# Splitting the two value projections over the last inverse levels, and reading the first head's sum ahead of the last inverse part

## What is computed

```python
# group A, per chunk of 64 tokens: needs the inverse of a unit lower triangular matrix
L = jnp.where(strict, jnp.einsum("bhncd,bhnsd->bhncs", k_beta, k) * decay, 0.0)
sol = lax.linalg.triangular_solve(L + eye, rhs, left_side=True, lower=True, unit_diagonal=True)
# group B, per head
z = jnp.einsum("bhqd,bhkd->bhqk", q_blk, kh) * scale
log_keep = jnp.where(mask, jax.nn.log_sigmoid(-z), 0.0)
between = lax.cumsum(log_keep, axis=3, reverse=True) - log_keep
weight = jnp.where(mask, jnp.exp(jax.nn.log_sigmoid(z) + between), 0.0)
return jnp.einsum("bhqk,bhkd->bhqd", weight, vh)
```

## Time and profile before

| what | us |
|---|---|
| median of 3 runs | 1599.32 |
| lowest and highest of them | 1590.52, 1599.54 |
| the profiled execution | 1589.53 |
| its span, as the trace has it | 1587.7 |
| TensorE busy in it | 1519.0 |

### The profile page before, as it was taken

One profiled execution on the slowest core, in us unless ns is written; L12 is line 12 of the kernel. 1 busy time (PEld: TensorE's weight loads), 2 busy tenths in 40 slices (PEclk: granted clock), 3 DMA queues, 4 the chain that ended last, 5 costly groups with the idle time before them and its releaser, 6 DMA issues.

```text
span 1587.7 us, 54543 instructions
## 1 busy us (share of the span) xinstructions
PE 1519.0 (96%) x25973; PEld 1334.5 (84%) x25973; DVE 258.1 (16%) x489; ACT 179.0 (11%) x383; POOL 143.7 (9%) x167
## 2 busy tenths in 40 slices
PE   9999999999999999999999999999999998999997
PEld 8787587777687864999999999999999998998996
DVE  3433310000143435100010010010010000000102
ACT  3223120000131332200000000000000000000001
POOL 2334200000022532200000000000000000000000
PEclk9999999999999999999999999999999999999999
DMA  9213344444243135999999999999999999999992
GB/s 329 95 54 134 106 160 159 160 159 147 80 173 107 53 144 207 364 397 373 373 379 369 354 369 376 370 383 368 371 363 377 364 384 359 367 359 369 399 374 97
DMA packets 133612, 433.48 MB, mean 273 GB/s; under 512 B 9082, under 2 KB 33916, under 8 KB 119052
## 3 DMA queue, kind: packets, MB, share of 16 engines
q1 hardware_dynamic: 132384, 427.70, 71.7%
q0 software_dynamic: 672, 2.14, 0.5%
q10 hardware_dynamic: 332, 0.13, 0.0%
HBM read 428.89 MB, written 1.05 MB: 271 GB/s over the span
## 4 chain that ended last, share of the span: by engine, by line
PE 92%; issue 3%; DVE 2%; ACT 1%; POOL 1%; DMA 0%; ACTq 0%; DVEq 0%
PE ps L1130 35%; PE ps L1154 18%; PE ps L979 9%; PE ps L681 8%; PE ps L990 4%; PE ps L844 3%; PE ps L692 3%; PE ps L1187 2%; PE ps L801 1%; PE ps L1059 1%; PE ps L677 1%; PE ps L811 1%; PE ps L707 1%; PE ps L714 1%; PE ps L821 1%
## 5 line engine op out<-in xcount | busy, mean ns | idle before, releaser
L1154 PE MATMUL ps<-LT_sb,ring 128*64 128x88 f32 x5376 | 217.5, 239 | 12.1 <-issue 10.7
L1130 PE MATMUL ps<-AT_sb,ring 128*64 128x88 f32 x5376 | 215.9, 239 | 10.6 <-issue 10.2
L1154 PEld LDWEIGHTS ps<-LT_sb,ring 128*64 128x64 f32 x5376 | 211.8, 137 | 16.9 <-issue 14.7
L1130 PE MATMUL ps<-wpost,ring 128*64 128x88 f32 x5376 | 216.6, 239 | 9.4 <-issue 7.9
L1130 PEld LDWEIGHTS ps<-AT_sb,ring 128*64 128x64 f32 x5376 | 211.5, 138 | 14.4 <-issue 13.7
L1130 PEld LDWEIGHTS ps<-wpost,ring 128*64 128x64 f32 x5376 | 210.8, 138 | 14.2 <-issue 11.7
L979 PEld LDWEIGHTS ps<-hT_sb,ring 128*128 128x128 f32 x768 | 136.0, 190 | 24.6 <-issue 9.1
L979 PE MATMUL ps<-hT_sb,ring 128*128 128x256 f32 (+1 forms) x768 | 155.7, 362 | 0.0
L681 PE MATMUL ps<-hT_sb,ring 128*128 128x256 f32 x576 | 129.7, 383 | 0.0
L681 PEld LDWEIGHTS ps<-hT_sb,ring 128*128 128x128 f32 x576 | 109.3, 192 | 15.5 <-DVE late L1632 0.5
L1976 POOL TENSOR_SCALAR small<-small 128x1 f32<-128x1 f32 x16 | 3.9, 241 | 1193.8 <-ACT late L1510 926.1
(11 more groups left out here) (284 smaller groups left out, 1163.7 us busy)
## 6 DMA issues: line engine op xcount, KB each, us to landing
ring<-in_moe_w_gate SPq DMA_DIRECT2D x84, 1024.0 KB, 8.1
ring<-in_moe_w_up SPq DMA_DIRECT2D x84, 1024.0 KB, 7.9
ring<-in_moe_w_down SPq DMA_DIRECT2D x84, 1024.0 KB, 7.8
late<-in_moe_w_up SPq DMA_DIRECT2D x28, 1024.0 KB, 8.2
late<-in_moe_w_gate SPq DMA_DIRECT2D x28, 1024.0 KB, 7.6
late<-in_moe_w_down SPq DMA_DIRECT2D x28, 1024.0 KB, 8.2
ring<-in_ffn_w_gate SPq DMA_DIRECT2D x11, 1024.0 KB, 5.4
ring<-in_ffn_w_up SPq DMA_DIRECT2D x11, 1024.0 KB, 8.1
```

Source lines behind the costliest of these rows:

```text
L1130: ins = mm(o[lo:lo + P // 2, :], pairs[:, m % 2, lo:lo + P // 2], xgT[e % 2][:, k, :], start=(k == 0 and m % 4 == 0), stop=(k == KD - 1), ...
L1154: ins = mm(o[lo:lo + P // 2, :], d[:, i, m * P + lo:m * P + lo + P // 2], moe_hid[:, 2 * j + i, :], start=(first and m % 4 == 0), stop=las ...
```

## The change

Six edits, the same for both layers:

```diff
@@ block.tensor
                 for l in range(LEVELS):
                     level_product(L, l, 0)
+                    if l == 1:
+                        project(L, S_FILL + l)
                     level_product(L, l, 1)
...
-                    project(L, S_FILL + l, ks=range(KD) if l < LEVELS - 1 else range(0, 2))
+                    if l < LEVELS - 2:
+                        if l != 1:
+                            project(L, S_FILL + l)
+                    else:
+                        project(L, N_STEPS - 2, ks=range(0, 4) if l == LEVELS - 2 else range(4, KD))
                     sb_cumsum(L, l)
...
                 per_head(0, lambda h: XT[:, h, :], lambda h: bv[:, h, :], vnew_ps)
-                project(L, N_STEPS - 1, ks=range(2, 5))
+                project(L, N_STEPS - 1, ks=range(0, 4))
                 pe.wait_ge(vnew_ready, 2 * L + 1)
                 per_head(1, lambda h: kend[:, h, :], lambda h: Vn[:, h, :], state_ps)
                 sb_cumsum(L, SB_H - 1)
-                project(L, N_STEPS - 1, ks=range(5, KD))
+                project(L, N_STEPS - 1, ks=range(4, KD))
@@ block.vector
                     V.tensor_tensor(X[:, s, :], bcm(ident, 4), bank(g).rearrange("p (a b) -> p a b", a=4),
                                     ALU.subtract).then_inc(X_ready, 1)
+
+                def inverse_first_left(g):
+                    s = slice(4 * g, 4 * g + 4)
                     V.tensor_tensor(XT[:, s, :], bcm(ident, 4), BT[:, s, :], ALU.subtract).then_inc(XT_ready, 1)
...
                     if l == 0:
                         inverse_first(0)
+                        inverse_first_left(0)
                         inverse_first(1)
                     sb_exponent(l)
+                    if l == 0:
+                        inverse_first_left(1)
@@ block.gpsimd
                 for l in range(LEVELS):
+                    if l == 1:
+                        sb_keep_mask(1)
                     if l and l + 1 < LEVELS:
                         blocks(l + 1, 0)
-                    sb_keep_mask(l)
+                    if l != 1:
+                        sb_keep_mask(l)
```

## The result

The changed kernel is slower: a ratio of 1.0048 to the kernel before, 95% interval 1.003 to 1.0066 (12 executions of each, in turns), which is +7.6 us (4.8 to 10.5) on 1592.35 us, the median of the kernel before in these rounds (single executions 1586.12 to 1599.54). It is a small difference, half a per cent, but the interval does not reach 1. The changed kernel's median is 1601.84 us (1592.61 to 1608.19), 9.5 us above the other median, its profiled execution 1592.61 us with a span of 1590.8 us.

What follows compares the result with a forecast made beforehand. TensorE's own work plus a few small-engine waits was taken to bound the mixers. Terms summed to +0.55 us a mixer, +2.1 with the clock, +4.2 for both: 1603.5 us against the 1599.3 median, range 1592 to 1608.

Steps and rivals of the forecast that it cites:

- What bounds the kernel, and that the loop's shift passes on: Mixers bound by TensorE's work plus small-engine waits; expert loop shifts by what they lose or gain; no DMA wait named.
- Levels 0 and 1: Head 1's scores wait 0.6 us instead of 1.71 and the clock stays up: -1.08 - 1.56 = -2.64 us a mixer.
- GpSimd's mask first is what keeps the cover: Head 1's sum: 0.45 us of cover if GpSimd masks before level 2's blocks; otherwise TensorE waits 0.6 to 2 us.
- Level 5: Four value products instead of eight take 3.43 us instead of 6.87: -3.43 us a mixer.
- Level 6: Head 6's functions stand behind step 23's copy on ScalarE; TensorE waits 4.5 us at the sum: +5.3 us a mixer.
- Behind the loop: Step 24: one product more covers head 7's 0.40 wait, +0.46 us; one more in the second part, +0.86 us.
- Sum of work and waits: Per mixer: -2.64 - 3.43 + 5.3 + 0.46 + 0.86 = +0.55 us, with 1.56 of clock gain at level 1 included.
- The clock: Behind head 6's new wait: a loss of 1.56 us taken, bounds 0 and 2.5; the loss moves from level 1 to level 6.
- if the mixers differ from each other: Sign that the forecast is wrong; both mixers run the same code and were expected to show the same waits.
- The absolute time: Whole kernel: +4.2 us on the median of the runs shown, 1599.3, gives 1603.5 us.
- the functions not held: Rival at level 6: head 6's functions get through in time; -3.96 us a mixer, -7.9 in all, 1591.4; chance 0.09.
- The clock costs more: Rival: level 0's 0.6 us wait still lowers the clock, or the new wait costs 2.5; up to 1607; chance 0.09.

Runs made afterwards that it cites:

- the copy later: Changed kernel, with ScalarE's copy of step 23 at level 6 behind head 6's functions instead of at the end of level 5; ratio 0.9959, 1585.19 us.
- 8, 3, 4, 1: Kernel before plus the edits at levels 0 and 1, value products at 8, 3, 4, 1 instead of 8, 2, 3, 3; ratio 0.9964.
- 7 and 1: Changed kernel with step 23 cut into 7 products on level 5 and 1 on level 6, not 4 and 4; mixer stretches 78.35 and 77.49 us.

## Why the prediction was right, and where it was not

**What bounds the kernel, and that the loop's shift passes on.** Right: the stretch between the mixers is 349.1 us in all six traces of the two kernels (from 168.15 to 517.28 in the one, 167.61 to 516.75 in the other), and behind the first gather the averages are the same. One reading was wrong: the view of waits does name a DMA, for line 629, 10.7 us into the run (1.9 us before, 1.7 in the changed kernel). It lies ahead of both mixers and changes nothing in the sum.

**Levels 0 and 1.** The scores wait 0.65 us, as forecast (0.6), and the rows behind it run at full clock at all twenty such places. From the scores to head 1's sum it takes 5.73 us against 5.45 forecast: the projection takes 3.65 instead of 3.45 and each half product 0.62 instead of 0.54. Why, no run shows. The step "GpSimd's mask first is what keeps the cover", with a wait of 0.6 to 2 us without it, was wrong: without it there is no wait. And the projection's move, costed at nothing, covers 0.38 us.

**Level 5.** Right: 137.15 - 133.71 = 3.44 us, no wait behind.

**Level 6.** Right in place, cause and size: 4.5 us forecast, 4.45 between the end of the products and the sum, with the copy 0.2 behind the products' end and the functions 0.9 behind the copy. The Trainium skill (page "TensorE: Matmul & The Clock Gate", section "Architectural detail: the array is 16× 32×32, not 1× 128×128") says that ScalarE's queue is strictly first in, first out. The trace agrees: the functions did not pass the copy, which started at 145.69 with the first of them at 146.59, and with the copy later they started at 140.58, ahead of it.

**Behind the loop.** Right: head 7's sum does not wait, from the products to it 4.33 us (4.49 forecast).

**Sum of work and waits.** Without any clock the forecast was 0.55 + 1.56 = +2.11 us a mixer. Measured, with the clock's losses out of both, 74.37 - 72.23 = +2.14. That they agree this closely is in part luck: the edits at levels 0 and 1 gave 0.72 (72.23 - 71.51) instead of 1.08, and the split cost 2.86 instead of 3.19, mostly because the place behind the loop took 1.05 more and not 1.32 (16.28 against 15.23 from the sum of head 6 to line 728).

**The clock.** This is the term that was mis-sized. The forecast moved one loss of 1.56 us from level 1 to level 6 and so set its change to zero. In fact the loss at level 1 comes in some stretches only, 1.05 on average, and the one behind the 4.3 us wait is 2.5 on average in the changed kernel, at most 3.9 there and 4.3 in the experiments; the prediction took 1.56, with 2.5 as its upper bound. The change of the clock's loss is so +1.5 a mixer (2.5 less 1.05) and not 0. A further one was not in the forecast at all: between the second mixer and the first gather the clock fell in all three traces of the changed kernel and in none of the kernel before, for 1.3 to 1.7 us, and not each time at the same place (see the last section). Nothing that the change touches stands there, it fell there in four of the eight experiments too, some without the long wait, and that the change brings it about is not shown. With +4.3 from waits and +4.5 from the clock, 8.8 us are accounted for; forecast were 4.2, and measured 7.6 (4.8 to 10.5). The premise that a wait of 1.2 us leaves the clock up held in the one trace that the prediction had read, and not in all.

**The sign "if the mixers differ from each other".** It came true: in the first trace of the changed kernel the mixers take 75.77 and 76.56, in the second 75.89 and 78.25. Their waits are the same, so the part of the forecast on waits stands, and what failed is the assumption of one fixed clock loss for both.

**The absolute time.** Forecast 1603.5, measured 1601.84, but the nearness owes something to chance: the median of the kernel before, 1599.3 in three executions, came out as 1592.35 in twelve, so the base was 7.0 us too high, while the two medians lie 9.5 us apart and not 4.2, 5.3 more.

**The rivals.** The one on the other side, the functions not held, was what the kernel with the later copy does: 1591.4 was worked out for a base of 1599.3, a gain of 7.9; measured is a gain of 6.5 us (3.8 to 9.1). "The clock costs more" was nearer the truth than the chance of 0.09 that it had, by its second half: the loss grew behind the new wait, not at level 0.

## What to carry to other kernels

When the work of one engine is cut or moved past a boundary, look up in the lists of the others what waits for its end, and what stands behind that waiting instruction: here a copy with no hurry of its own held three functions on the critical path, and moving it from the end of level 5 to the end of level 6 turned +0.5% into -0.4%. Cover a wait of 0.8 us by moving one product of 0.86 us, not by an even division. And count a wait on TensorE as the wait plus what the clock may take behind it: 0 or 1.6 us behind 1.7 us, 1.4 to 4.3 behind 4.3 us.

## What the runs showed of the hardware

The granted clock is not bound to a wait alone. Behind a wait of 1.7 us in the same place of the same program it fell in four of six stretches of the kernel before and not in the other two. Behind two waits of 1.21 and 0.87 us, which all kernels have behind each mixer, it fell at 6 of the 28 places (two mixers, fourteen traces), three of them behind the first mixer. The changed kernel and the second trace of the kernel before, TensorE from the same products on:

```profile
600.15 5.36 PE L844 MATMUL ps<-ring,hT_sb 128*128 128x512 f32 x8 [0.87 <-ACT hT_sb L1450]
605.35 0.60 PE L850 MATMUL ps<-cst,h_sb 128*128 128x128 f32 x4
```

```profile
597.46 0.60 PE L850 MATMUL ps<-cst,h_sb 128*128 128x128 f32 x4
597.90 7.03 PE L844 MATMUL ps<-ring,hT_sb 128*128 128x512 f32 x16
```

Eight rows take 5.20 us in the one, sixteen take 6.87 in the other. In four more traces (the changed kernel's second and third; 8, 3, 4, 1; 7 and 1) the fall came 36 us behind the wait of 0.87, in the routing. The changed kernel's second trace, then the second of the kernel before:

```profile
634.86 1.32 PE L649 MATMUL ps<-cst,x_sb 128*128 128x128 f32 x8 [0.32 <-DVE x_sb L1554]
...
637.53 3.67 PE L1036 MATMUL ps<-cst 128*128 128x512 f32 x4
640.99 0.21 PE L1054 MATMUL ps<-small,sbe 128*128 128x8 bf16 x1
```

```profile
629.79 1.98 PE L1030 MATMUL ps<-cst 128*128 128x512 f32 x4
```

The four rows take 3.46 us in the one and 2.03 (to 631.82) in the other. In the first of the two traces TensorE is busy for 6.53 of the 7 us from 630 to 637, at a granted clock of 1.00, and from 637 to 642 the clock is 0.66; from 604 us on, no wait above 0.32 us is marked ahead of the fall. So the length of the longest wait does not decide it: at twenty places with a wait of 0.65 us no loss followed, and here one came behind 0.32. The losses at these ten places are 1.3 to 1.7 us each. What decides them is not settled here. For a comparison of two kernels it means that a difference of some microseconds can lie in clock losses at places that the change never touched, and that one trace of each is too few to tell.
